# A two-layer attention encoder on one core: first loads in slices, last output pieces in half order

## What is computed

```python
for l in range(2):                                  # DEPTH = 2, SEQ = D_MODEL = 1024
    h = rms_norm(x, norm_g[l])
    z = einsum('bsd,de->bse', h, w_in[l])           # 7 parts: q, k, v twice, gate
    o_da = diff_attention(qd, kd, vd, lam, ...)     # 4 groups, softmax minus lam * softmax
    o_na = neighbourhood_attention(qn, kn, vn, rpb) # 4 groups, 2-D window with bias
    o = concatenate([o_da, o_na]) * silu(gate)
    x = x + einsum('bse,ed->bsd', o, w_out[l])
out = rms_norm(x, final_g)

def rms_norm(x, g): return x * rsqrt(mean(x * x) + 1e-6) * g
```

## Time and profile before

| | |
|---|---|
| three runs | 1502.69, 1508.54, 1509.71 us; median 1508.54 |
| profiled execution: its own time | 1503.38 us |
| its span | 1501.6 us |
| TensorE busy | 1437.1 us, 96% of the span |
| VectorE, ScalarE, GpSimd busy | 895.6, 684.9, 459.4 us |
| mean granted clock of TensorE | 0.99 |
| DMA | 79.41 MB, mean 53 GB/s |

### The profile page before, as it was taken

How to read it: one execution, slowest core, us unless ns; L and a number is a source line. 1 busy time by engine, 2 the same in 40 slices (tenths; PEclk the granted TensorE clock), 3 DMA queues, 4 the chain that set the end, 5 groups by cost and what they waited for, 6 DMA issues and landing times.

```text
span 1501.6 us, 24043 instructions
## 1 busy us (share of the span) xinstructions
PE 1437.1 (96%) x8160; PEld 1170.8 (78%) x8160; DVE 895.6 (60%) x1828; ACT 684.9 (46%) x1306; POOL 459.4 (31%) x370
## 2 busy tenths in 40 slices
PE   7999999999999999899999999999999999997994
PEld 6788787878787888677887878787788888876874
DVE  6666666767655555653436667766666555557323
ACT  5445455544444444542524544544544444445330
POOL 2322223223323232313633132312322323331261
PEclk9999999999999999999999999999999999999997
DMA  4700101021111110301110001010102111121012
GB/s 175 147 29 28 43 21 49 21 60 36 45 51 55 40 59 35 133 15 57 56 47 37 24 35 35 30 40 21 53 22 74 43 52 42 52 96 58 29 56 112
DMA packets 39246, 79.41 MB, mean 53 GB/s; under 512 B 18832, under 2 KB 18832, under 8 KB 39184
## 3 DMA queue, kind: packets, MB, share of 16 engines
q1 hardware_dynamic: 39184, 78.60, 15.7%
HBM read 66.57 MB, written 15.96 MB: 55 GB/s over the span
## 4 chain that ended last, share of the span: by engine, by line
PE 87%; DVE 4%; issue 3%; ACT 2%; SPq 2%; DMA 1%; POOL 0%; DVEq 0%; POOLq 0%; ACTq 0%
PE proj L932 18%; PE proj L934 17%; PE proj L933 17%; PE scores L968 9%; PE turn L1025 5%; PE mix L1077 3%; PE mix L1078 3%; PE mix L1042 2%; PE mix L1041 2%; PE mix L1043 2%; SPq L476 2%; PE scores L1025 2%; DVE prob L1356 1%; PE mix L1051 1%; ACT prob L797 1%
## 5 line engine op out<-in xcount | busy, mean ns | idle before, releaser
L932 PE MATMUL proj<-h_hi,w_hi 128*128 128x512 f32 x1184 | 501.2, 423 | 18.3 <-DVE h_lo L1265 10.1
L934 PE MATMUL proj<-h_hi,w_lo 128*128 128x512 f32 x1184 | 467.3, 395 | 0.0
L933 PE MATMUL proj<-h_lo,w_hi 128*128 128x512 f32 x1184 | 464.3, 392 | 0.0
L932 PEld LDWEIGHTS proj<-h_hi,w_hi 128*128 128x128 f32 x1184 | 223.4, 189 | 82.9 <-issue 36.0
L934 PEld LDWEIGHTS proj<-h_hi,w_lo 128*128 128x128 f32 x1184 | 223.1, 188 | 51.6
L933 PEld LDWEIGHTS proj<-h_lo,w_hi 128*128 128x128 f32 x1184 | 224.5, 190 | 34.3
L1356 DVE CUSTOM_DVE_ANT_0 prob<-scores,inner 128x1024 f32<-128x1024 f32 (+1 forms) x192 | 204.0, 1062 | 72.1 <-PE scores L968 71.4
L577 POOL TENSOR_TENSOR w_lo<-w_raw,w_hi 128x1024 fp32r<-128x1024 f32 x78 | 191.8, 2459 | 179.5 <-ACT w_hi L730 179.4
L1364 DVE TENSOR_TENSOR pt_lo<-turn,pt_hi 128x512 fp32r<-128x512 f32 x208 | 139.2, 669 | 152.5 <-ACT pt_hi L772 151.2
L772 ACT ACTIVATE pt_hi<-turn 128x512 fp32r<-128x512 f32 x208 | 120.5, 579 | 224.4 <-PE turn L1025 223.6
L797 ACT ACTIVATE prob<-prob,nm,escale_now 128x1024 f32<-128x1024 f32 x128 | 158.0, 1235 | 3.3 <-DVE nm L1360 3.2
(11 more groups left out here) (162 smaller groups left out, 2248.8 us busy)
## 6 DMA issues: line engine op xcount, KB each, us to landing
w_raw<-chunks SPq DMA_DIRECT2D x81, 512.0 KB, 3.2
mixed_dram<-gate SPq DMA_DIRECT2D x28, 256.0 KB, 2.0
edge<-bias_dram SPq DMA_DIRECT2D x32, 224.0 KB, 3.8
h_lo<-mixed_dram SPq DMA_DIRECT2D x14, 512.0 KB, 7.5
xt<-x_t SPq DMA_DIRECT2D x8, 512.0 KB, 9.1
bias_dram<-bias_rows SPq DMA_DIRECT2D x16, 240.0 KB, 5.8
out_t<-prob SPq DMA_DIRECT2D x6, 512.0 KB, 3.0
out_t<-gate SPq DMA_DIRECT2D x2, 512.0 KB, 3.0
```

Source lines behind the costliest of these rows:

```text
L932: pe.matmul(dst, a_hi, b_hi, start=start, stop=False)
L933: pe.matmul(dst, a_hi, b_lo, start=False, stop=False)
L934: return pe.matmul(dst, a_lo, b_hi, start=False, stop=stop)
```

## The change

**Head.** The first two row tiles' worth of chunks 0 and 1 (`HEAD = 2`) and the first half of x's row 0 are loaded by transfers of their own, row 1 stands ahead of the chunks' remaining six tiles, and the norm gains are loaded from ScalarE's queue. ScalarE and VectorE make the `_hi` and `_lo` parts in the same slices. The integer table `dist`, that stood first on VectorE, comes behind the first slices. The squares run two rows behind `h_hi`, their sums three rows behind `h_lo`. TensorE waits for the slices, and `sum_squares` stands in the middle of the first Q piece.

**End of the last layer.** The order is `HALVES_LAST`: 8, 9, 0 to 7, then 10, 12, 14 (first halves), 11, 13, 15 (second halves). That needs three chunks at once, so chunk 6 goes to the buffers `wq_hi`, `wq_lo`. Sum, `stat`, `rinv`, spread and result of the first half run among the pieces of the second. The second half's sum takes the last square as a second matmul into the same column, without GpSimd's addition. The result is made in place in `xt`, in halves, and stored in 16 transfers of 256 KB.

```diff
+    HEAD = 2
+    HALVES_LAST = LATE[:10] + [10, 12, 14, 11, 13, 15]
+    THIRD = LAST_ROWS + 1
+    CHUNKS_LAST = {0: LAST_ROWS, 1: THIRD, 2: THIRD + 1, 6: NT}
...
+        def out_weights(l, j):
+            if l + 1 == DEPTH and j == THIRD:
+                return wq_hi, wq_lo
+            return w_hi[:, out_buffer(l, j)], w_lo[:, out_buffer(l, j)]
...
-            sp.dma_start(w_raw[:], chunks[0].rearrange("p (t c) -> p t c", c=P)).then_inc(w_in, 16)
-            sp.dma_start(ngain[:], norm_gain).then_inc(gain_in, 16)
-            for i in range(NT):
+            sp.dma_start(w_raw[:, 0:HEAD], w0[:, 0:HEAD]).then_inc(head_in, 16)
+            sp.dma_start(xt[:, 0, half(0)], x_t[0:P, half(0)]).then_inc(half_in, 16)
...
-            for i in range(NT):
-                sp.wait_ge(norm_done, i + 1)
-                sp.dma_start(out_t[i * P:(i + 1) * P, :], normed[i % 4]).then_inc(stored[i % 4], 16)
+            for hf in range(2):
+                for i in range(NT):
+                    sp.wait_ge(norm_done, hf * NT + i + 1)
+                    sp.dma_start(out_t[i * P:(i + 1) * P, half(hf)], xt[:, i, half(hf)]).then_inc(stored, 16)
...
+            act.dma_start(ngain[:], norm_gain).then_inc(gain_in, 16)
+            act.wait_ge(head_in, 16)
+            act.activation(w_hi[:, 0, 0:HEAD], w_raw[:, 0:HEAD], ACT.Copy).then_inc(head_hi, 1)
...
+            for i in range(2, NT):
+                act.wait_ge(x_in[i], 16)
+                h_hi_part(0, i)
+                square_row(i - 2)
...
+                if last and j == THIRD:
+                    reached(act, pv_done, DEPTH * MIXES)
...
+            def sum_half(hf):
+                done = squared(DEPTH + 1) - 3 if hf == 0 else squared(DEPTH + 1) - 1
+                pe.wait_ge(sum_done, done)
+                if hf:
+                    pe.wait_ge(sq_done, squared(DEPTH + 1))
...
+                    if hf:
+                        last = pe.matmul(part, square[:, cols], ones[:], start=False, stop=True)
...
+                            if k == HEAD:
                                 pe.wait_ge(w_lo_done, c + 1)
...
+                    first_q(l, q_ts[0], range(0, 4))
                     sum_squares(l)
-                    first_q(l, q_ts[0])
+                    first_q(l, q_ts[0], range(4, NT))
...
+                    odd = HALVES_LAST[-3:]
+                    out_piece(l, odd[0], range(0, 6))
+                    sum_half(0)
+                    out_piece(l, odd[0], range(6, 8))
+                    out_piece(l, odd[1], range(0, 4))
+                    spread_half(0)
+                    out_piece(l, odd[1], range(4, 8))
+                    out_piece(l, odd[2], range(NT))
+                    sum_half(1)
+                    spread_half(1)
...
+            norm_stats(DEPTH)
+            add_piece(DEPTH - 1, EARLY + end - 3, HALVES_LAST[end - 3])
+            normed(0, range(0, 4))
+            add_piece(DEPTH - 1, EARLY + end - 2, HALVES_LAST[end - 2])
+            normed(0, range(4, NT))
+            add_piece(DEPTH - 1, EARLY + end - 1, HALVES_LAST[end - 1])
+            norm_stats(DEPTH + 1)
+            normed(1, range(NT))
```

More of the change, by code:

```diff
@@ L327, in hybrid_encoder @@
         gain_in = sem("gain_in")
-        second_in = sem("second_in")
+        second_in = [sem(f"second_in{i}") for i in range(2)]
+        head_in = sem("head_in")
+        half_in = sem("half_in")
+        head_hi = sem("head_hi")
+        head_lo = sem("head_lo")
+        half_hi = sem("half_hi")
+        half_lo = sem("half_lo")
         lam_loaded = sem("lam_loaded")
@@ L337, in hybrid_encoder @@
         mixed_in = [sem(f"mixed_in{i}") for i in range(NT)]
-        stored = [sem(f"stored{b}") for b in range(len(normed))]
+        stored = sem("stored")
         made = sem("made")
@@ L882, in _ @@
                 wq_hi_part(l)
+                if l == 0:
+                    for i in range(NT - 2, NT):
+                        square_row(i)
                 if l == 0:
@@ L1101, in out_piece @@
                         pe.wait_ge(h_ready, l * HR + NT + k + t % 2 + 1)
-                    b = out_buffer(l, chunk_of(t))
-                    last = three(out_bank(out_number(0, t) - IN), w_hi[:, b, k], w_lo[:, b, k], h_hi[:, k, half(t)],
+                    hi, lo = out_weights(l, chunk_of(t))
+                    last = three(out_bank(l, n - l * PPL - IN), hi[:, k], lo[:, k], h_hi[:, k, half(t)],
                                  h_lo[:, k, half(t)], start=k == 0, stop=k == end - 1)
@@ L1170, in spread, with spread_half @@
                 last.then_inc(spread_mm, 1)
+            def sum_half(hf):
[3 more added lines that the diff above has]
+                    pe.wait_ge(sq_done, squared(DEPTH + 1))
+                for i in range(hf * NT // 2, (hf + 1) * NT // 2):
+                    part, cols = mix[:, i:i + 1], slice(i * P, (i + 1) * P)
+                    last = pe.matmul(part, squares[:, cols], ones[:], start=True, stop=hf == 0)
+                    if hf:
+                        last = pe.matmul(part, square[:, cols], ones[:], start=False, stop=True)
+                last.then_inc(stat_mm, 1)
+            def spread_half(hf):
+                pe.wait_ge(rinv_done, DEPTH + hf + 1)
+                for i in range(hf * NT // 2, (hf + 1) * NT // 2):
+                    last = pe.matmul(scores[:, 0, i * P:(i + 1) * P], rinv[:, i:i + 1].to_broadcast([P, P]), ident[:],
+                                     start=True, stop=True)
+                last.then_inc(spread_mm, 1)
             def first_part(l, ts, ks, hi, lo):
@@ L1245, in _ @@
                     for t in LATE[-2:]:
-                        last = three(out_bank(out_number(0, t) - IN), w_hi[:, b, k], w_lo[:, b, k], h_hi[:, k, half(t)],
+                        last = three(out_bank(l, out_number(0, t) - IN), w_hi[:, b, k], w_lo[:, b, k], h_hi[:, k, half(t)],
                                      h_lo[:, k, half(t)], start=k == 0, stop=k == NT - 1)
@@ L1280, in _, with w_lo_slice, first_row @@
                     dve.tensor_tensor(squares, squares, (square_b, square)[i % 2 == 0], ALU.add).then_inc(sum_done, 1)
+            def w_lo_slice(b, raw, ts):
+                return dve.tensor_tensor(w_lo[:, b, ts], raw[:, ts], f32(w_hi[:, b, ts]), ALU.subtract)
+            def first_row(hf):
+                return dve.scalar_tensor_tensor(h_lo[:, 0, half(hf)], xt[:, 0, half(hf)], ngain[:, 0:1],
+                                                f32(h_hi[:, 0, half(hf)]), ALU.mult, ALU.subtract)
+            dve.wait_ge(head_hi, 1)
+            w_lo_slice(0, w_raw, slice(0, HEAD)).then_inc(head_lo, 1)
+            dve.wait_ge(half_hi, 1)
+            first_row(0).then_inc(half_lo, 1)
+            dve.wait_ge(h_hi_done, 1)
+            first_row(1).then_inc(h_ready, 1)
+            dve.wait_ge(head_hi, 2)
+            w_lo_slice(1, second_raw, slice(0, HEAD)).then_inc(head_lo, 1)
+            dve.wait_ge(dist_int, 1)
+            dve.scalar_tensor_tensor(dist, dist_table, -1.0, dist_table, ALU.mult, ALU.min).then_inc(consts_done, 1)
+            h_lo_part(0, 1)
+            dve.wait_ge(w_hi_done, 1)
+            w_lo_slice(0, w_raw, slice(HEAD, NT)).then_inc(w_lo_done, 1)
+            dve.wait_ge(w_hi_done, 2)
+            w_lo_slice(1, second_raw, slice(HEAD, NT)).then_inc(w_lo_done, 1)
+            for i in range(2, NT):
+                h_lo_part(0, i)
+                if i > 2:
+                    sum_row(i - 3)
+            for i in range(NT - 3, NT):
+                sum_row(i)
             def lam_dots():
```

135 lines of the change are left out of this document (82 added, 53 removed).

## The result

| | before | after |
|---|---|---|
| median | 1508.54 us (9 runs, 1502.69 to 1511.05) | 1498.21 us (9 runs, 1496.47 to 1502.37) |
| ratio of after to before, 95% interval | | 0.9938 [0.9923, 0.9953] |
| profiled execution, its span | 1503.38, 1501.6 us | 1502.37, 1500.6 us |

The change makes the kernel 10.3 us faster by the medians, 0.6% or 9.4 us by the ratio; the forecast was 1497.0. The two profiled executions differ by 1.0 us only: the one of before is nearly its fastest, the one of after its slowest. A profile is one draw, so I compare it stretch by stretch and say where other executions of the same code came out otherwise.

A forecast was written before the change was run, and what follows sets the result against it. TensorE, busy for 96% of the span, was taken to bound the kernel. Head 2.6 plus end 8.9 gave 11.5 us off the profiled 1503.38, 1491.9; the median's 5.2 above its profile made 1497.0, range 1489 to 1502.5.

The forecast's parts named there:

- The signs for "right": Across the trace: first matmul before 6.5 us, bias transfers at 35.3, idle 3.6, last add at 1475.8, span 1490.1.
- The first matmul: At the start: a smaller first load lets TensorE begin at 5.6 to 5.8 us, 4.3 us earlier.
- TensorE's own shift: At the start: TensorE's work moves 3.8 us earlier, after 0.5 us of waiting at row 2.
- SyncE's chain: Chunk 3, bias transfers, chunk 5 and the transpose at 73.71 move 2.6 us earlier, less than TensorE's 3.8.
- The squares that lag hold none of this up: At the remaining six rows: ScalarE and VectorE each stay below TensorE's 2.7 us a row, so lagging squares delay nothing.
- Rival B: At about 70 us: the longer idle drops TensorE's clock; head brings 0.8, total gain 9.7 us, 1498.8; chance 0.2.
- the likeliest case: Whole kernel: head and end gains arrive in full, 11.5 us off, median 1497 us; chance 0.57.
- rival E: Idles between groups: clock falls cost 1.8 us each, over six eat the gain, eleven give 1517; chance 0.04.
- The end: Behind the last pieces: the end comes at 1492.7 us, a gain of 8.9, between 7.2 and 10.3.
- The covers: Before the last pieces: chunk 8 is ready 1.3 us early and the thirteenth addition 0.5 us early, so TensorE doesn't wait.
- rival C: At the end: chunk 8 or thirteenth sum late, TensorE stands 2 to 4 us; 1501 to 1502.5; chance 0.12.
- Rival D: At the start: first slice lands with the rest at 7.4 us, head brings nothing; gain 8.9, 1499.6; chance 0.07.

The follow-up runs named there:

- e1: Only the head of the change (slices, gains on ScalarE's queue, lagging squares) on the kernel before: 1508.05 us, ratio 0.9999.
- e2: Only the end of the change (second halves last, three chunks at once, half stores) on the kernel before: 1500.53 us, ratio 0.995.
- e7: Kernel after, with each square directly behind its row's h_hi and each sum behind its h_lo, slices kept: single time 1498.57 us.
- e11: Kernel after, TensorE's first group of layer 0 written out, 12 unread matmuls in the idle before the transpose at 72 us: 1497.53 us, ratio 0.9935.
- e3: Kernel after, with six of the 16 bias transfers issued between the loads of chunks 2 and 3: 1496.6 us, ratio 0.9921.
- e4: Kernel before, with six of the 16 bias transfers issued between the loads of chunks 2 and 3: 1507.73 us, ratio 1.0001.
- e5: Kernel before, with one bias transfer more, repeated into a table row nobody reads, so chunk 5 is issued later: one time, 1511.43 us.
- e6: Kernel after, with the norm gains loaded from SyncE's queue again, second there: single time 1500.22 us.
- e9: Kernel after, with 12 unread matmuls meant for the idle before the transpose at 72 us, placed one step too early: 1496.7 us, ratio 0.9936.
- e12: Kernel after, with TensorE's first group of layer 0 written out ahead of its loop, without extra matmuls: 1499.75 us, ratio 0.9941.

## Why the prediction was right, and where it was not

**The profiled execution.** The signs for "right" that name places late in the trace failed: the last add was forecast at 1475.8 and came at 1485.03, the span at 1490.1 and was 1500.6. The 10.5 us are 3.6 at the head, 4.7 in the middle and 2.2 at the end. That the median came within 1.2 us of 1497.0 is in part luck: the gains of e1 and e2 add up to 7.5 us, which would be 1501.0.

**The first matmul.** Forecast 5.6 to 5.8, measured 6.71, and 5.93 to 6.77 in the other executions of the new head. The step that failed is the landing: I had the half row in SBUF at 4.2, by 512 KB having been split at 4.21; it was taken up at 5.06. Two transfers one behind the other (issued at 0.86 and 1.32) did not land like one of more bytes. TensorE's own shift was to be 3.8; the idle at 68.61 moved to 66.22, 2.4. Of the missing 1.4 us, 1.0 stands at the first matmul already, most of it the landing; the rest is waits for the next rows (0.53 and 0.29 us, forecast 0.5 in all). The old head scatters too: its first matmul came at 8.46, 10.04, 10.05 and 10.49 in four executions.

**SyncE's chain.** Forecast 2.6 earlier, measured 1.7. The mechanism was right: chunk 3's landing became the late one (ScalarE waited 0.93 us for it at 32.37), and that was 3.1 us behind its issue, forecast 3.2. What was off is the split of chunk 2, "found at 25.7 again" and in fact at 26.80. The lagging squares wait for VectorE's sums, three times, as ScalarE's rows show:

```profile
19.97 1.06 ACT L755 ACTIVATE prob<-xt 128x1024 f32<-128x1024 f32 x1 [0.56 <-DVE prob L1377]
...
22.31 1.06 ACT L755 ACTIVATE prob<-xt 128x1024 f32<-128x1024 f32 x1 [0.23 <-DVE prob L1377]
...
24.64 1.07 ACT L755 ACTIVATE prob<-xt 128x1024 f32<-128x1024 f32 x1 [0.23 <-DVE prob L1377]
```

"The squares that lag hold none of this up" was wrong by that, 1.0 us, though e7 shows that without the lag it would have been worse. The idle follows from the two shifts: 2.39 + 2.39 - 1.67 = 3.1; forecast 3.6.

**The clock.** Rival B, with a chance of 0.2, is what happened; the likeliest case was wrong here. The fall cost 2.7 us in three executions, the changed kernel's profile among them, and 1.5 to 1.6 in three others, around the 1.8 that I had put it at the earlier trace rows. I weighed one idle of 2.21 that lost the clock against one of 2.39 that kept it, but both are shorter than the 3.6 us that I forecast myself; six of six executions with an idle over 3.1 us fell. And the trace of before had more to read: behind idles of 2.67 at 621.70, 2.20 at 631.19 and 2.10 at 1379.36 the clock fell, behind 2.09 at 649.13 and 2.67 at 1353.10 it stayed. With the two that I took, four of seven fell; 0.2 was too low. The 2.67 are also longer than the 2.39 that rival E calls "as long as any between groups". The head was worth 1.7 less 2.7 in the trace and 0 in e1. The Trainium skill, TensorE: Matmul & The Clock Gate, section Why this matters for your kernels, names gaps between bursts of matmuls as what costs the clock. The traces agree: with the gap filled (e11) or shortened to 1.3 us (e3) the loss is gone.

**The end.** Forecast 8.9. The pieces moved by 2.6 instead of 1.7 (in nine other executions 1.8 to 2.3), the tail took 15.6 instead of 14.3. Term by term, forecast and measured: sums 2.05 and 2.6, power 1.0 and 1.02, spreads 1.9 and 2.1, eight results 4.9 and 5.4, last store with its tail 2.7 and 2.7. Two terms were mis-sized. The sums began at 0.22 us a pair and went to 0.43 from 1487.7 on, where the granted clock falls to 0.50; in e3 they ended before it fell, and took 1.8. The results take 0.67 us at half the width, not half of the time between two full ones, 0.60. (A slip besides: the low end of this term, given as 7.2, adds up to 7.0.) The fit in the Trainium skill, SBUF — State Buffer, section The DMA setup-cost knee, gave 0.6 us more for the last store; the trace has 2.7 us from the last result (1497.9) to the span's end (1500.6), the sum from rows. What I did not see is that the old end scatters too: in e1 and e4 its sixteen sums took 3.5 us at the lower clock and not 2.05,

```profile
1483.54 3.54 PE L1190 MATMUL mix<-ones,prob 128*128 128x1 f32 x16 [3.42 <-POOL prob L678]
```

and anchor to end was 77.0 and 77.1 us, in e5 75.7. The new end took 67.4 to 68.8 in the eight executions that have it without extra matmuls in the tail (after, e2, e3, e6, e7, e9, e11, e12). So the gain is 6.7 to 9.7, e2's ratio says 7.5, and 8.9 is within it, a little high. The parts of the end (the order in halves, the square summed by TensorE, the 16 stores) were not run one by one; what each is worth is read from the rows only.

**The covers** held: splits and additions of rival C were in time but for 0.45 us once, with 0.5 us to spare by the forecast. Rival D did not occur: the first slices were taken up at 3.84 and 5.06, not at 7.4. Of rival E, the idles between groups (1.2 to 1.4 us) kept the clock; those at the layer's turn and ahead of the last group lost it more often in this profile than in before's, but not as an effect of the change, as the next paragraphs show.

**The sum.** 0.8 for the head with the clock lost, as rival B has it, and the end gives 1498.8; 1498.21 was measured. The point forecast, 1497.0, is near too, though the head was over-sized by about 2.6 and the two halves run alone give 7.5, not 11.5. The offset between profile and median was carried along as a guess: before's execution lies 5.2 us below its median, the changed kernel's 4.2 above.

**The middle.** The 4.7 us lost between landmark and anchor are scatter of code that did not change. In the 14 traces this part took 1273.4 to 1273.7 us three times (before, e7, e11), 1275.3 once (e9) and 1276.7 to 1278.6 ten times, with the old end (e1, e4, e5) as with the new: before's profile is one of the rare short ones. Of the 4.7, 2.8 arise at the layer's turn (622 to 809 us), 0.6 in the groups behind it and 1.4 ahead of the last group (1357 to 1367). At 651 to 654 the clock was 1.00 in before's execution and 0.56 in after's, each behind an idle of 2.09 us (after first, then before).

```profile
651.32 0.69 PE L1084 MATMUL turn<-ident,prob 128*128 128x128 f32 x2 [2.09 <-DVE pt_lo L1491]
```

```profile
651.00:654.00 3.00, 2.68 (x8) 2.14 (x8) 1.94 (x5) 2.27 (x5) 0.29 (x1) 0.56 0.00 0
```

```profile
649.13 0.44 PE L1021 MATMUL turn<-ident,prob 128*128 128x128 f32 x2 [2.09 <-DVE pt_lo L1364]
```

```profile
651.00:654.00 3.00, 2.88 (x20) 2.40 (x21) 2.77 (x6) 0.00 (x0) 0.04 (x1) 1.00 0.00 0
```

The second place, after, behind an idle of 2.67 us; before's clock was 1.00 behind the same idle:

```profile
1359.00:1362.00 3.00, 3.00 (x18) 2.82 (x18) 1.53 (x2) 0.30 (x1) 0.00 (x0) 0.62 0.16 63
```

**Open.** Why the clock stays down longer in one execution than in another after a like idle (2.7 us against 1.6), why an idle of 2.1 to 2.7 us keeps the clock at one time and not at another, and whether filling the idle is worth its 2.7 us in the median (e9, e11 don't show it).

## What to carry to other kernels

When a change makes the critical engine arrive earlier at something that another queue delivers, work out both shifts: the difference is a longer idle, and here an idle that grew from 2.4 to 3.1 us cost as much time by its clock as the head had won, or more. Look for what stands ahead of the late transfer on its queue (here bias transfers that could go into an earlier wait) before you shorten anything in front of it. And before you compare two profiles, ask which part of their difference lies in code that did not change: here 4.7 us, against 1.0 for the whole.
